# Four more gate panels as block products ahead of the attention, four fewer threaded through it

## The reference

```
proj = rmsnorm(x) @ w_in            # q | six k/v streams | nsa gates | u | v | merge gates (2 x 2048)
o_a  = nsa_attention(q, k/v, gates) # 16 heads, 4 groups; compressed, selected and window branch
o_b  = spatial_gating(gelu(u), gelu(v))
g    = sigmoid(merge gates)         # 512 x 2 x 2048
x    = x + (g[A] * (o_a @ w_proj_a) + g[B] * (o_b @ w_proj_b)) @ w_mix_out
x    = x + cross attention;  x = x + SwiGLU;  final rmsnorm
```

## Time and profile before

| what | value |
|---|---|
| median of three runs | 2768.27 us (2766.99 to 2770.83) |
| the profiled execution, its own time | 2769.71 us |
| its span, first to last instruction | 2767.9 us |
| granted TensorE clock, mean | 0.997 |
| block products, first to last load | 143.48 to 320.78 us |
| phases c, k, v, g | 320.78 to 485.86 us |
| attention with the threaded panels | 485.86 to 805.01 us |

### The profile page before, as it was taken

One profiled execution on the slowest core, in us unless ns is written; L12 is line 12 of the kernel. 1 busy time (PEld: TensorE's weight loads), 2 busy tenths in 40 slices (PEclk: granted clock), 3 DMA queues, 4 the chain that ended last, 5 costly groups with the idle time before them and its releaser, 6 DMA issues.

```text
span 2767.9 us, 37969 instructions
## 1 busy us (share of the span) xinstructions
PE 2724.2 (98%) x14157; PEld 2306.6 (83%) x14157; DVE 2082.3 (75%) x2998; ACT 1184.9 (43%) x1903; POOL 449.3 (16%) x414
## 2 busy tenths in 40 slices
PE   8999999999999999999999999999999999999998
PEld 7888888888888888888877888888888888788886
DVE  6777653667655555555678899999999998988887
ACT  6344311766640322211144555555555555443334
POOL 0000020545530555411000100000000000000000
PEclk9999999999999999999999999999999999999999
DMA  7488662332223445544334788988888888999982
GB/s 242 133 186 179 168 147 66 86 95 58 58 82 105 107 121 147 146 117 118 102 126 129 180 206 203 217 205 215 201 221 201 217 198 259 307 288 302 296 267 92
DMA packets 636920, 469.92 MB, mean 170 GB/s; under 512 B 14180, under 2 KB 580312, under 8 KB 630872
## 3 DMA queue, kind: packets, MB, share of 16 engines
q1 hardware_dynamic: 564352, 412.39, 50.5%
q0 software_dynamic: 54736, 34.61, 9.5%
q10 hardware_dynamic: 17672, 20.77, 2.4%
HBM read 406.64 MB, written 61.08 MB: 169 GB/s over the span
## 4 chain that ended last, share of the span: by engine, by line
PE 83%; DVE 5%; ACT 4%; DMA 2%; issue 2%; POOL 2%; SPq 1%; ACTq 0%; DVEq 0%; POOLq 0%
PE banks L967 10%; PE banks L1406 9%; PE banks L1403 9%; PE banks L969 9%; PE banks L968 9%; PE banks L1404 9%; PE banks L1468 4%; PE banks L1469 4%; PE banks L1470 4%; PE banks L1065 2%; PE banks L1068 2%; PE banks L1066 2%; PE banks L1234 1%; PE banks L1236 1%; PE banks L1235 1%
## 5 line engine op out<-in xcount | busy, mean ns | idle before, releaser
L1485 DVE CAST w_hi<-raw 128x512 fp32r<-128x512 f32 (+1 forms) x264 | 154.1, 584 | 307.7 <-PE banks L969 234.1
L967 PE MATMUL banks<-act_hl,w_hi 128*128 128x512 f32 (+1 forms) x944 | 375.6, 398 | 4.4 <-DVE w_lo L1506 2.4
L968 PE MATMUL banks<-act_hl,w_hi 128*128 128x512 f32 (+1 forms) x944 | 370.1, 392 | 0.0
L969 PE MATMUL banks<-act_hl,w_lo 128*128 128x512 f32 (+1 forms) x944 | 369.9, 392 | 0.0
L1404 PEld LDWEIGHTS banks<-t_hl,wf_lo 128*128 128x128 f32 x1312 | 246.5, 188 | 58.1
L1406 PE MATMUL banks<-t_hl,wf_hi 128*128 128x512 f32 x656 | 259.5, 396 | 0.0
L1403 PE MATMUL banks<-t_hl,wf_hi 128*128 128x512 f32 x656 | 259.4, 395 | 0.0
L1404 PE MATMUL banks<-t_hl,wf_lo 128*128 128x256 f32 x1312 | 257.8, 278 | 0.0
L1947 DVE TENSOR_TENSOR wf_lo<-raw_f,wf_hi 128x1024 fp32r<-128x1024 f32 x164 | 200.4, 1222 | 55.9 <-ACT wf_hi L2604 55.8
L2604 ACT ACTIVATE wf_hi<-raw_f 128x1024 fp32r<-128x1024 f32 x164 | 173.8, 1060 | 137.2 <-PE banks L1406 81.6
L1404 PEld LDWEIGHTS banks<-tok_hl,wf_lo 128*128 128x128 f32 x984 | 184.8, 188 | 43.7
(11 more groups left out here) (361 smaller groups left out, 6172.8 us busy)
## 6 DMA issues: line engine op xcount, KB each, us to landing
raw_f<-in_w_ffn_in_dram SPq DMA_DIRECT2D x82, 1024.0 KB, 9.1
raw<-in_w_in_dram SPq DMA_DIRECT2D x50, 1024.0 KB, 5.6
h_full<-hidden_blocks SPq DMA_DIRECT2D x35, 1024.0 KB, 7.9
wo_raw<-in_w_ffn_out_dram SPq DMA_DIRECT2D x32, 1024.0 KB, 10.1
hidden_blocks<-tok_hl SPq DMA_DIRECT2D x44, 512.0 KB, 6.3
s<-in_w_ffn_in_dram SPq DMA_DIRECT2D x40, 512.0 KB, 6.3
s<-in_w_ffn_in_dram POOLq DMA_DIRECT2D x40, 512.0 KB, 6.5
raw_g<-in_w_in_dram SPq DMA_DIRECT2D x18, 1024.0 KB, 8.8
```

The lines of the kernel that those rows point to most:

```text
L967: pe.matmul(dst, w_hi[:, q, j, 0:m], hi, start=first, stop=False)
L968: pe.matmul(dst, w_hi[:, q, j, 0:m], lo, start=False, stop=False)
L969: return pe.matmul(dst, w_lo[:, q, j, 0:m], hi, start=False, stop=last)
```

## The change

`G_TILES` gets two more pairs of merge gate panels, so 11 pairs in place of 9, and `GATES_AHEAD` goes from 16 to 20, so the phase `merge` has 12 panels and not 16. Since the units go round three weight buffers, the last unit now falls on another buffer, and ScalarE's wait ahead of phase `c` is for one unit more.

```diff
-G_TILES = [("q", n) for n in range(0, 8, 2)] + [("merge", n) for n in range(PLAIN_GATES, PLAIN_GATES + 10, 2)]
+G_TILES = [("q", n) for n in range(0, 8, 2)] + [("merge", n) for n in range(PLAIN_GATES, PLAIN_GATES + 14, 2)]
 G_PAIRS = len(G_TILES)
-GATES_AHEAD = PLAIN_GATES + 10
+GATES_AHEAD = PLAIN_GATES + 14
...
-assert G_PAIRS % 2 == 1 and (7 * G_PAIRS - 1) % 3 == 2
+assert G_PAIRS % 2 == 1 and (7 * G_PAIRS - 1) % 3 == 1
...
                     if g < G_UNITS:
                         g_unit_high(g)
                     else:
-                        act.wait_ge(g_unit, G_BASE + G_UNITS - 2)
+                        act.wait_ge(g_unit, G_BASE + G_UNITS - 1)
                         high(PH["c"], 0, 0, g - G_UNITS)
```

## The result

The changed kernel takes 2789.47 us (median of 4 runs, 2787.3 to 2790.15) against 2769.41 (4 runs, 2766.99 to 2770.83): a ratio of 1.0072, 95% interval 1.0057 to 1.0086. It is 20 us slower. The profiled execution took 2789.09 us, with a span of 2787.4, 19.5 us longer than the one before.

The account below looks back on a forecast made before the run. The kernel was taken as bound by TensorE's issue time plus its waits. Four panels -43.5, two pairs +39.0 and attention waits +16.5 summed to +12.0 us, giving 2780 us, range 2765 to 2790.

Parts of the forecast that it names:

- The matrix work: TensorE: four gate panels leave the attention, -43.5 us; two more pairs of block products, +39.0 us; in all -4.5 us.
- The later wait ahead of phase c, cost 0: ScalarE's later write of quarter 0 of c is covered by VectorE's joins: cost 0, uncovered at most 1 us.
- The attention gives back less than its tiles: Attention: chains on slower engines don't shrink with TensorE's steps, so waits grow by 16.5 us, from 3 to 27.
- The factor: Attention: 0.7 of the 23.4 us sum, because part of each chain, up to the coefficients, follows TensorE.
- the weighings: Attention: they wait a step for ScalarE's copy and VectorE's low part; shorter steps cost 3 us more.
- Block 3: Attention, query block 3: GpSimd's scaling stays fixed, eight half-units lose 0.79 us each, 6.3 us.
- Block 2: Attention, query block 2: third transposes need all four wide rows from GpSimd; 1.0 x 8 = 8 us lost.
- Block 0: Attention, query block 0: six tiles leave the last six half-units without shortening them; 4.1 us stay as waiting.
- Columns decide: Rival: attention chains shorten with TensorE's steps, waits grow by under 4.5 us, kernel at 2764 to 2768; 14%.
- half hidden: Rival: waits grow by 4.5 to 10 us, kernel at 2768 to 2774; 19%.
- Fixed and more: Rival: everything fixed, exponentials end last, waits grow by 23 to 32 us, kernel at 2787 to 2796; 13%.
- The clock: Rival: longer waits lower the granted clock in the attention, five times for 9 us, kernel at 2789; 2%.

Follow-up runs that it names:

- blocks_only: Changed kernel with eleven pairs of block products but still 16 threaded panels in the attention, four panels computed twice: 2811.02 us, ratio 1.0158.
- thread20: Kernel before, taken the other way: seven pairs of block products and 20 threaded panels, nothing left out: 2768.71 us, ratio 1.0002.
- attn8_only: Kernel before with nine pairs and only eight threaded panels, eight gate panels filled by copies instead of computed: 2734.91 us, ratio 0.9877.
- coef_first_after: Changed kernel with VectorE making a half-unit's coefficients ahead of the maximum of the next half-unit's first step: 2789.41 us, ratio 1.0076.
- narrow_before: Kernel before with GpSimd scaling only the first 128 columns of each wide row of probabilities: 2764.80 us, ratio 0.9991.

## Why the prediction was right

Slower was forecast, at 2780 us within 2765 to 2790; 2789.5 came, at the edge of the range and above the forecast's own 2774 to 2787. Direction and mechanism were right, but two misses point the same way: the 12.0 us of the sum became 19.5 (profiled executions) by 5.8 us more in the attention and 3.2 ahead of it, less 1.5 in the other stretches. Nothing was forecast for the 3.2, so that the time still fell inside the range is partly luck. Its steps:

- *The matrix work.* Right: four panels 43.5 us; two pairs +38.6 us where 39.0 was said. `blocks_only` alone has it at +38.5.
- *The later wait ahead of phase c, cost 0.* Right: phase c's 43.31 us are unchanged. *"The phases behind it move as one"*: wrong by 3.2 us. The burst of loads already left a gap, and with two more pairs it is 5.46 for 2.57 us: 4.8 to 5.5 us in all five profiled kernels with eleven pairs and this order of loads, against 2.6 to 3.0 in the five with nine. That the gap comes from the burst is shown, and that 0.7 us of the growth are slower splits beside GpSimd; why the weights land 2.2 us later is open (with seven pairs, in `thread20`, the gap was 3.36, so it isn't the count alone).
- *The attention gives back less than its tiles.* The mechanism was right and the size off. The term was 0.7 x 23.4 = 16.5 us (16.4 to be exact); measured are 22.3, so nearly all of the 23.4, and loads waited 37.6 us where about 29 were said. Two parts were mis-sized. The factor took three tenths of every chain, the part up to the coefficients, as following TensorE. Measured as in the earlier trace rows, from the first scores of the next half-unit to the end of a half-unit's coefficients, this part takes on average by block 2.51, 1.92, 2.35 and 2.14 us before and 2.80, 2.05, 1.97 and 1.63 after: it did shrink in blocks 2 and 3, and grew in blocks 0 and 1. And the weighings were put at 3 us (2.1 with the factor), while the waits for the low part grew by 7.7. So the sum of the fixed chains comes near 22.3 although its terms don't; `attn8_only` lies near it too.
- *By block.* Block 3: 6.3 us as fixed chain, measured 16.3 - 10.0 = 6.3. That match is luck: of the 6.9 us by which loads waited longer there, 2.9 are for GpSimd's scaling, which was meant, and 4.0 for the low part. Block 2: 8, measured 10.9 - 5.0 = 5.8, all for GpSimd. Block 1: 2, measured 3.2, by waits for the low part. Block 0: 4.1, measured 5.4 + 1.5 = 6.9: a half-unit that doesn't shrink was foreseen, one that grows was not. Its loads waited 5.7 us longer for GpSimd and 1.2 for the low part. Below, blocks 0 and 2 of the kernel before: ScalarE, the fourth busy time, is at 33.0 of 41.2 us in the one and 55.5 of 79.7 in the other; in block 0 it has the least room, and its order (panel copy, store, queries, then the copy for the weighing) held the low part back in the half-unit shown.

```profile
485.86:527.07 41.21, 40.26 (x242) 33.57 (x241) 29.28 (x143) 32.99 (x128) 23.30 (x43) 1.00 0.29 73
...
606.61:686.26 79.65, 78.29 (x454) 66.89 (x452) 57.11 (x180) 55.52 (x162) 44.26 (x48) 1.00 0.30 76
```

The half-unit that follows the one shown, in the changed kernel, shows how coefficients come late:

```profile
559.75 0.62 ACT L2206 ACTIVATE w_hi<-raw 128x512 fp32r<-128x512 f32 x1
560.40 0.69 DVE L1506 TENSOR_TENSOR w_lo<-raw,w_hi 128x512 fp32r<-128x512 f32 x1 [1.81 <-ACT w_hi L2206]
561.83 0.17 DVE L1726 TENSOR_TENSOR coef<-coef,gates 128x6 f32<-128x6 f32 x1
562.09 0.80 POOL L2803 TENSOR_SCALAR prob_c<-prob_c,coef 128x32 f32<-128x32 f32 x2 [4.59 <-DVE coef L1726]
562.95 0.11 PEld L1188 LDWEIGHTS banks<-ident,prob_c 128*32 128x32 f32 x2 [1.86 <-POOL prob_c L2803]
```

The scores began at 558.19. VectorE stood 1.81 us for ScalarE's split of threaded gate weights, made their low part, and only then took the maximum and made the coefficients, 3.8 us behind the scores; the transposes waited 1.86 us. So here the threaded work's own splits lengthened the chain. That this is the rule in block 0 was not tested.

- *Rivals.* Columns decide (14%) and half hidden (19%): excluded, the extra waiting is 22.3 us and not under 4.5 or 10. Fixed and more (13%) is nearly what happened, with the gap's 3.2 us on top. The clock (2%): it did not fall in this attention, but fell in two others, with 8 panels and with the coefficients first. The rule to relieve the busiest engine would have said -4.5 us; TensorE was relieved of 4.9 us and the kernel lost 20.

## What to carry to other kernels

Work threaded through a latency-bound stage costs little up to the point where it fills the stage's chains, and taking it out gives back only what lies over them: here 87% of a panel's time at 20 panels, 49% at 16 and 25 to 36% at 12. Before moving such work to a place where it is 10% cheaper, compare the stage's length per step with its chain (first trigger to last release on the slower engines), and take the whole chain as fixed for a first estimate: here that sum came within 1.1 us, while a discount for queues that shrink with the moved work was 5.8 us too low. Check it block by block, since errors of single chains can cancel. When a chain is shortened and the stage isn't, look at the waits by releaser: they show whether the next chain, or the same engine's next instruction, has taken its place.

## What the runs showed that I had not expected

The granted clock fell to 1.2 GHz inside the attention with waits shorter than the 2.4 us of the earlier trace rows: in `coef_first_after` for 3.4 us, with no wait over 1.7 us in that attention, and in `attn8_only` for 3.4 us at 500.3, with no wait over 1.2 us in the 5 us ahead of it. Its second fall there, 6.8 us from 524.2, came within a wait of 3.0 us. In the changed kernel, with waits up to 1.9 us, it stayed at 2.4 GHz throughout. And the fall behind a gap is not certain: `narrow_before` had its gap of 2.83 us ahead of phase k and no fall, which made that stretch 163.7 us instead of 165.1.
